# A hybrid decoder layer: hand-overs and last job by token tile, columns by transposes, halved final stores

## What is computed

```python
mod = silu(c) @ w_ada + b_ada          # six groups of D: shift1, scale1, gate1, shift2, scale2, gate2
u = x * (1 + scale1) + shift1
h = u @ w_in                            # inputs of three branches (conv, gated DeltaNet, attention) and their gates
m = sum(sigmoid(g_i) * (y_i @ P_i))     # merge of the three branches
x = LN(alpha * x + gate1 * (m @ w_o))   # first norm, then
u = x * (1 + scale2) + shift2           # (ln1's gain and bias and scale2, shift2 are folded into one multiply and add)
h = relu(u @ w_ff1) ** 2                # D_FF = 8192
x = LN(alpha * x + gate2 * (h @ w_ff2)) # the output
```

## Time and profile before

| what | us |
|---|---|
| median of 3 runs (2622.71, 2624.74, 2627.75) | 2624.74 |
| the profiled execution, its own time | 2627.94 |
| its span (first to last event in the trace) | 2626.2 |
| PE busy / DVE busy / ACT busy / POOL busy | 2554.2 / 1721.4 / 1172.5 / 84.4 |
| mean granted clock of PE | 0.983 |
| HBM traffic | 534.68 MB read, 205 GB/s over the span |

### The profile page before, as it was taken

One profiled execution on the slowest core, in us unless ns is written; L12 is line 12 of the kernel. 1 busy time (PEld: TensorE's weight loads), 2 busy tenths in 40 slices (PEclk: granted clock), 3 DMA queues, 4 the chain that ended last, 5 costly groups with the idle time before them and its releaser, 6 DMA issues.

```text
span 2626.2 us, 33584 instructions
## 1 busy us (share of the span) xinstructions
PE 2554.2 (97%) x12200; PEld 2086.3 (79%) x12200; DVE 1721.4 (66%) x2318; ACT 1172.5 (45%) x1453; POOL 84.4 (3%) x89
## 2 busy tenths in 40 slices
PE   7888999999999999999999999999999999999997
PEld 3567888788878887888788888878788888888886
DVE  4677766786678757776667667766665645546556
ACT  2146354635463545535444434434454354453442
POOL 0001010101001100110000000000000000000000
PEclk8799999999999999999999999999999999999999
DMA  9865657656666567556787877877565665666654
GB/s 311 308 202 161 179 170 223 184 175 181 199 208 176 161 190 237 168 148 181 235 263 239 268 255 238 265 234 254 155 183 190 226 184 191 191 186 194 186 190 137
DMA packets 300174, 540.05 MB, mean 206 GB/s; under 512 B 39152, under 2 KB 44784, under 8 KB 298736
## 3 DMA queue, kind: packets, MB, share of 16 engines
q1 hardware_dynamic: 270752, 522.29, 63.7%
q10 hardware_dynamic: 29264, 15.68, 2.0%
HBM read 534.68 MB, written 3.21 MB: 205 GB/s over the span
## 4 chain that ended last, share of the span: by engine, by line
PE 50%; DVE 1%; ACT 0%; DMA 0%; issue 0%; DVEq 0%; ACTq 0%
PE acc L1725 49%; PE bank L1728 1%; PE bank L1725 0%; DVE z_lo L1095 0%; DVE w_lo L1110 0%; DMA raw<-in_w_in 0%; DVE xr L1101 0%; DVE x L1101 0%; DVE macc L1101 0%; ACT w_hi L647 0%; DVE stats L1594 0%; DVE xr L1095 0%; DVE ff_part L1095 0%; DVE gated L1557 0%; DVE merged L1559 0%
## 5 line engine op out<-in xcount | busy, mean ns | idle before, releaser
L1110 DVE TENSOR_TENSOR w_lo<-raw,w_hi 128x1024 fp32r<-128x1024 f32 x800 | 982.3, 1228 | 686.6 <-ACT w_hi L647 642.4
L647 ACT ACTIVATE w_hi<-raw 128x1024 fp32r<-128x1024 f32 x792 | 835.7, 1060 | 1134.8 <-PE acc L1725 823.1
L1725 PE MATMUL acc<-w_hi,u_hi 128*128 128x512 f32 x2304 | 921.7, 400 | 21.9 <-DVE w_lo L1110 18.7
L1725 PE MATMUL acc<-w_hi,u_lo 128*128 128x512 f32 x2304 | 903.0, 392 | 0.0
L1725 PE MATMUL acc<-w_lo,u_hi 128*128 128x512 f32 x2304 | 902.1, 392 | 0.0
L1725 PEld LDWEIGHTS acc<-w_hi,u_hi 128*128 128x128 f32 x2304 | 435.6, 189 | 120.5 <-DVE w_lo L1110 22.9
L1725 PEld LDWEIGHTS acc<-w_hi,u_lo 128*128 128x128 f32 x2304 | 435.3, 189 | 93.0
L1725 PEld LDWEIGHTS acc<-w_lo,u_hi 128*128 128x128 f32 x2304 | 436.2, 189 | 86.2 <-issue 1.0
L1725 PE MATMUL acc<-w_hi,z_hi 128*128 128x512 f32 x896 | 350.9, 392 | 3.7 <-DVE mod L1095 3.7
L1725 PE MATMUL acc<-w_hi,z_lo 128*128 128x512 f32 x896 | 349.4, 390 | 0.0
L1725 PE MATMUL acc<-w_lo,z_hi 128*128 128x512 f32 x896 | 349.3, 390 | 0.0
(11 more groups left out here) (247 smaller groups left out, 1470.1 us busy)
## 6 DMA issues: line engine op xcount, KB each, us to landing
raw<-in_w_in SPq DMA_DIRECT2D x416, 512.0 KB, 4.5
raw<-in_w_ff SPq DMA_DIRECT2D x256, 512.0 KB, 4.3
raw<-in_w_ada SPq DMA_DIRECT2D x192, 512.0 KB, 4.7
raw<-in_w_branch_a SPq DMA_DIRECT2D x32, 512.0 KB, 4.8
raw<-in_w_branch_b SPq DMA_DIRECT2D x32, 512.0 KB, 4.9
raw<-in_w_branch_c SPq DMA_DIRECT2D x32, 512.0 KB, 4.8
raw<-in_w_o SPq DMA_DIRECT2D x32, 512.0 KB, 4.7
IT<-decay_d ACTq DMA_DIRECT2D x8, 512.0 KB, 6.5
```

The costliest lines, as they stand in the source:

```text
L647: a.activation(w_hi[:, u % PARTS, :, :], raw[:, rl % RAWS, :, :], ACT.Copy).then_inc(hi_ready.sem, 1)
L1110: v.tensor_tensor(w_lo[:, u % PARTS, :, :], raw[:, rl % RAWS, :, :] if src is None else src, w_hi[:, u % PARTS, :, :], ALU.subtract).then_ ...
L1725: return t_.matmul(dst, lhsT, rhs, start=start, stop=stop)
```

## The change

- `mod` groups, 8 in the passes and 8 in the merge: PE transposes the four 128 x 128 blocks of `macc` (four `turn`), and DVE sums 128 values for each of 4 columns (`sum_turned`, a `tensor_reduce` into the new tile `mcol`) ahead of the addition. The groups of the first stage (`first_columns`) stay as they are.
- `gate_rows` uses `turn` too. The second `gate_rows` moves from after the last W_o job to slot 24 of the stage (AT_GATE2).
- Merge: the wait for `mod_set` moves behind the next slots.
- First pass: `load_decay` moves ahead of the exponential of the heads; AT_DECAY is 48 instead of 50.
- `by_tile` replaces `last_units`: all 8 units of the job first for token tile 0, then for tile 1. It is used for the last W_o job, the first FF1 job and the last FF2 job. Its units find their halves by `weights(n)`: for two jobs from the last W_o job on, the first 4 units of each lie in `zw_hi`, `zw_lo` (over z_hi, z_lo, unused then); in the last FF2 job in `uw_hi`, `uw_lo` (over u_hi, u_lo). `slot_free(n)` lets these units be converted 4 units earlier.
- The hand-over goes by token tile: `turn_xhat(m, n)` transposes 4 k tiles of one token tile into a bank (tile 0 during the second half of the last W_o job, tile 1 during the first half of the first FF1 job), `make_u2` on ACT makes all of u2 (4 activations of 128 x 128 per group), `make_lo` on DVE its lower half.
- Tail: the last two passes over the columns and the stores are done in two halves of 1024 columns.

```diff
+N_OUT = (J_OUT + NCH - 1) * UPJ
+N_LAST = (J_FF + FFQ * FF_JOBS - 1) * UPJ
...
-AT_SMALL, AT_SUMS, AT_DECAY = KT + 1, 40, 50
+AT_GATE2 = 24
+AT_SMALL, AT_SUMS, AT_DECAY = KT + 1, 40, 48
...
+        uw_hi = sb("uw_hi", [P, PARTS, UK, NC], F32R, at=u_at)
+        zw_hi = sb("zw_hi", [P, PARTS, UK, NC], F32R, at=tmp_at)
...
+        def weights(n):
+            if N_OUT <= n < N_OUT + 2 * UPJ and n % UPJ < PARTS:
+                return zw_hi[:, n % PARTS, :, :], zw_lo[:, n % PARTS, :, :]
+            if N_LAST <= n < N_LAST + PARTS:
+                return uw_hi[:, n % PARTS, :, :], uw_lo[:, n % PARTS, :, :]
+            return w_hi[:, n % PARTS, :, :], w_lo[:, n % PARTS, :, :]
+
+        def slot_free(n):
+            return n + 1 - (PARTS if N_OUT <= n < N_OUT + 2 * UPJ or n >= N_LAST else 0)
...
                 if i == 0:
+                    act.wait_ge(decay_out.sem, 16)
+                    load_decay()
                     act.wait_ge(N["decay_left"].sem, 1)
                     activate(heads[:, 4, :, :], heads[:, 4, :, :], ACT.Exp, "heads_made", 1)
...
-                if i == 0:
-                    act.wait_ge(decay_out.sem, 16)
-                    load_decay()
...
+            out_to(AT_GATE2 + 1)
+            gate_rows(1, gate2_b, 0)
+            gate_rows(1, gate2_b, 2)
...
+            def make_u2(m, n):
+                g = NCH * m + n
+                act.wait_ge(N["xhat_turned"].sem, g + 1)
+                if m:
+                    act.wait_ge(N["u2_lo"].sem, n + 1)
+                for q in range(BPC):
+                    k = BPC * n + q
+                    activate(u2[n][:, q, :], bank[n][:, q * P:(q + 1) * P], ACT.Identity, *(("u2_made", g + 1) if q == BPC - 1 else ()),
+                             scale=lnc[:, 0, k:k + 1], bias=lnc[:, 1, k:k + 1])
+                o.after()
+                activate(u_hi[:, BPC * n:BPC * (n + 1), m * P:(m + 1) * P], u2[n][:, :, :], ACT.Copy, "u2_hi", g + 1)
+
+            first_ff = NCH * UPJ
+            out_unit(first_ff)
             root(0, 0)
+            out_unit(first_ff + 1)
+            out_unit(first_ff + 2)
+            make_u2(0, 0)
+            out_unit(first_ff + 3)
+            make_u2(0, 1)
+            out_unit(first_ff + 4)
+            make_u2(0, 2)
             root(0, 1)
+            out_unit(first_ff + 5)
+            make_u2(0, 3)
+            out_unit(first_ff + 6)
+            out_unit(first_ff + 7)
+            for n in range(NCH):
+                make_u2(1, n)
...
+            def sum_turned(n, b):
+                o.do(v.tensor_reduce(mcol[:, n % 2, :], b[:, :].rearrange("p (b c) -> p b c", c=P), mybir.AxisListType.X, ALU.add))
+                o.after()
+                return mcol[:, n % 2, :]
...
+            residual(0)
+            inverse_root(0, 0)
+            for n in range(NCH):
+                xhat(0, n)
+            for n in range(3):
+                out_unit(first_ff + n)
+            make_lo(0, 0)
+            out_unit(first_ff + 3)
+            make_lo(0, 1)
+            residual(1)
+            out_unit(first_ff + 4)
+            make_lo(0, 2)
+            inverse_root(0, 1)
+            xhat(1, 0)
+            xhat(1, 1)
+            out_unit(first_ff + 5)
+            make_lo(0, 3)
+            out_unit(first_ff + 6)
+            xhat(1, 2)
+            xhat(1, 3)
+            out_unit(first_ff + 7)
+            make_lo(1, 0)
...
+                for h in range(2):
+                    cs = slice(h * D // 2, (h + 1) * D // 2)
+                    stt(xr[:, m, cs], xr[:, m, cs], aggr[:, m, 0:1], ln_g[:, cs], ALU.subtract, ALU.mult)
+                    o.after()
+                    stt(x1[:, m, cs], xr[:, m, cs], rstd[:, m:m + 1], ln_b[:, cs], ALU.mult, ALU.add, "out_made", 2 * m + h + 1)
...
-            def last_units(n, dst, left):
+            def by_tile(n, dst, j, left, side):
                 hi, lo = left
                 for m in range(MT):
                     ms = slice(m * P, (m + 1) * P)
-                    for v in range(PARTS):
+                    for v in range(UPJ):
                         if m == 0:
                             pe.wait_ge(lo_ready.sem, n + v + 1)
+                        if n == J_FF * UPJ and v % 2 == 0:
+                            pe.wait_ge(N["u2_lo"].sem, NCH * m + v // 2 + 1)
...
+                        side(m, v)
...
-                        last = mm(bank[MOD_BANK[n]][:, b:b + 1], macc[:, n % 2, b * P:(b + 1) * P], ones[:, 0:1])
+                        last = turn(bank[MOD_BANK[n]][:, b * P:(b + 1) * P], macc[:, n % 2, b * P:(b + 1) * P])
...
                 if n == MMODS - 1:
-                    pe.wait_ge(N["mod_set"].sem, FIRST_GROUPS + n)
                     for t in range(6):
                         next_slot((MERGES - 1) * 4 * UPJ + KT + 2 * t + 2 - count[0])
+                        if t == 0:
+                            pe.wait_ge(N["mod_set"].sem, FIRST_GROUPS + n)
                         turn_merged(t)
...
-                        last = mm(bank[n][:, b * P:(b + 1) * P], mod[:, k:k + 1].broadcast_to([P, P]), ident[:, :])
+                        last = turn(bank[n][:, b * P:(b + 1) * P], mod[:, k:k + 1].broadcast_to([P, P]))
...
+            def out_side(m, v):
+                if (m, v) == (1, 3):
+                    pe.wait_ge(N["gate_made"].sem, 2 * NCH)
+                if m and 3 <= v < 3 + NCH:
+                    turn_xhat(0, v - 3)
+
+            by_tile(N_OUT, 1, (J_OUT + NCH - 1) // 2 + 1, (u_hi, u_lo), out_side)
+
+            def ff_side(m, v):
+                if m == 0 and v in (5, 7):
+                    turn_xhat(1, v - 5)
+                    turn_xhat(1, v - 4)
+
+            by_tile(J_FF * UPJ, 0, J_FF // 2 + 1, (u_hi, u_lo), ff_side)
...
+                        by_tile(N_LAST, 1, (J_FF + FFQ * FF_JOBS - 1) // 2 + 1, (z_hi, z_lo), lambda m, v: None)
```

More of the change, by code:

```diff
@@ L253, in layer_program @@
         w_lo = sb("w_lo", [P, PARTS, UK, NC], F32R)
+        u_at = top[0]
         u_hi = sb("u_hi", [P, KT, S], F32R)
@@ L1044, in _ @@
                     o.begin(i, 60)
-                count = [0]
+                count = [0 if i else UK * (UPJ - LEAD)]
                 next_slot = slots(i, FF_JOBS * UPJ, J_FF * UPJ, FF_JOBS * UPJ, R_FF, plain_place, count)
                 if i == 0:
[L1048 to L1062, removed]
                     o.begin(0, 60)
@@ L1079, in _ @@
                                  *(("h_hi", j + 1) if h else ()))
-                while count[0] < FF_JOBS * KT - (2 * LEAD if i == FFQ - 1 else 0):
+                while count[0] < (FF_JOBS - (2 if i == FFQ - 1 else 0)) * KT:
                     next_slot()
+                if i == FFQ - 1:
+                    for u in range((FF_JOBS - 2) * UPJ + LEAD, FF_JOBS * UPJ):
+                        r = i * FF_JOBS * UPJ + u
+                        hi_unit(J_FF * UPJ + r, u, 16 * ((R_FF + r) // RAWS + 1), u)
                 o.end(FFQ if i == FFQ - 1 else 0)
@@ L1590, in _, with variance @@
             o.begin(0, 200)
-            def normalise(which, m, cols):
+            def variance(m, which=0):
                 o.do(v.bn_stats(stats[:, m, NCH - 1, :], xr[:, m, cols]))
@@ L1617, in _, with residual @@
                 o.after()
-            out_to(AT_HALF + 2)
+            out_unit(first_ff - 1)
             cols = slice((NCH - 1) * NC, NCH * NC)
-            for m in range(MT):
+            def residual(m):
                 if m:
@@ L1683, in _ @@
                         break
-                    while count[0] < (j + 1) * KT:
-                        next_slot()
+                    if i < FFQ - 1 or j < FF_JOBS - 2:
+                        while count[0] < (j + 1) * KT:
+                            next_slot()
+                    else:
+                        for u in range(j * UPJ + LEAD, FF_JOBS * UPJ - 1):
+                            lo_unit((i * FF_JOBS + J_FF) * UPJ + u, u, u)
                     job_wait(dve, i * FF_JOBS + (J_FF + j))
@@ L1697, in _ @@
                 if i == FFQ - 1:
-                    while count[0] < FF_JOBS * KT - 2 * LEAD:
-                        next_slot()
+                    u = FF_JOBS * UPJ - 1
+                    lo_unit((i * FF_JOBS + J_FF) * UPJ + u, u, u)
                 o.end(FFQ if i == FFQ - 1 else 0)
@@ L2130, in _ @@
                 for b in range(BPC):
-                    last = mm(bank[n % 4][:, b:b + 1], macc[:, n % 2, b * P:(b + 1) * P], ones[:, 0:1])
+                    last = turn(bank[n % 4][:, b * P:(b + 1) * P], macc[:, n % 2, b * P:(b + 1) * P])
                 last.then_inc(N["mcol_summed"].sem, 1)
@@ L2159, in _, with turn_xhat @@
             gate_rows(0, 2 * KT)
[L2160 to L2161 removed]
+            next_slot(AT_GATE2 - count[0])
             gate_rows(1, 5 * KT)
[L2163 to L2174 removed]
+            next_slot((NCH - 1) * KT - count[0])
+            def turn_xhat(m, n):
+                pe.wait_ge(N["xhat_made"].sem, NCH * m + n + 1)
+                if m:
```

(8 more changed lines are left out.)

139 lines of the change are left out of this document (56 added, 83 removed).

## The result

| what | before | after |
|---|---|---|
| median of 4 runs, us | 2623.72 (2621.99 to 2627.75) | 2600.82 (2600.38 to 2601.19) |
| profiled execution, its own time | 2627.94 | 2600.64 |
| its span | 2626.2 | 2598.9 |
| mean granted clock of PE | 0.983 | 0.986 |

The ratio is 0.9909, 95% interval 0.9893 to 0.9924: faster by 22.9 us. The forecast was 2598.5, in a range of 2590.5 to 2608.

The account below looks back on a forecast made before the run. PE, busy 97% of 2626.2 us, was taken to bound the kernel, almost all of it matmul issue. The terms summed to -26.3 us: 2601.6 for a profiled execution, 2598.5 for a median, range 2590.5 to 2608.

Parts of the forecast that it names:

- C: Mod columns by transposes in passes and merge: 0.46 us less PE per group against 0.7 more DVE, sum -3.4 us.
- A: First pass, earlier decay load: normalised KC ready about 3.9 us sooner, PE's hole cut to 2 us, worth -5.5 us.
- D: Gate rows by transposes instead of fp32 products: first gate 3.49 to 1.75 us on PE, worth -1.75 us.
- E: Hand-over, last W_o job and first FF1 job by token tile: job start to first ReLU shortened, worth -7.3 us.
- I take no fall: First pass: PE's clock would not drop behind the remaining 2 us hole before KC.
- B: Merge, wait for DVE's mod columns moved: removes PE's 3.68 us wait and 1.6 of slow clock, -5.3 us.
- Rival 1: Passes: DVE takes over, reductions delay late weight units; total gain only -19.5, so 2605.2 us; chance 0.12.
- Rival 2: Mod columns, gate rows, hand-over: transposes save nothing on PE; total gain only -15.9, so 2608.8 us; chance 0.07.
- Rival 3: Rows of transposes count as idling, three clock falls of 1.6 us; total -21.5, so 2603.2 us; chance 0.05.
- Rival 4: Hand-over becomes a ping-pong of PE and ACT waits, +22 us there; total -4, so 2620.5 us; chance 0.03.
- Rival 5: By-tile jobs: weight supply starves first tiles, units 6.6 us in series; slower, about 2661 us; chance 0.03.
- F: Tail, last job by token tile with half passes and half stores: tile 1 starts sooner, last store shorter, -3.1 us.

Follow-up runs that it names:

- the repair: The changed kernel with all DVE subtractions of the decays in the first pass done before the next two weight units; 2598.61 us.

## Why the prediction was right, and where it was not

**The total.** The terms summed to -26.3; the profiled pair moved by 27.3, of which 1.9 belongs to no edit, so the change itself gave 25.4. The median came 2.3 us above the forecast: I carried the profiled execution's excess of 3.2 us over to the new kernel as a constant, while the new kernel's profile lay at its median. That the sum came so close is in part luck: C gave 1.0 more than forecast, while A fell 1.3 short, D and E 0.7 and the last job 0.5.

**A, 1.3 too high.** The failed step is "I take no fall". The hole was 2 us as forecast, and the clock fell to half for some 3 us. The ground for that step was one execution, and a row that shows too little: the 2.48 us idle in 170 to 175 are the part inside the window of a single wait of 2.94 us, behind which the clock falls in most runs (last section). The run with the same hole and no fall prices it: between KC and the macc group PE is there 1.5 us sooner, of which 0.8 is given back at the next tight unit (it waits 1.32 instead of 0.73), so 0.7 net. The other 0.6 is DVE: I had w_lo ready at 257.3, its subtraction only started at 257.29, and it was ready at 258.5. Expecting DVE to be 6 us earlier behind KC was too much (its last work ahead of the reduction began 4.9 earlier, 254.30 for 259.22); the bound (-3.3 to -8.9) held.

**B** gave 5.42 for 5.3. The undoing showed 6.9, for a reason outside the sum: C lengthens the wait that B removes.

**C.** The late groups gave 0.47 each. The reduction from PSUM took 0.69 us on average over 16, as the one from SBUF that I took for it (0.68), so neither bound was needed. Of the first groups, two cost +0.8 as forecast (+0.7), while the one in pass 4 gained 0.46: two waits there, 0.24 and 0.59, became one of 1.15. The reading behind the term was loose too: PE waits 0.62 us at 540.96 and 0.59 at 1096.39, but at 818.58 only 0.20. Rival 1 (2605.2) is out for C, since the second groups cost nothing on DVE and the first ones 1.2 us where the forecast itself had 2.1; only A moved towards its 3.3.

**D and E, 0.7 too high together.** Gate rows: 1.66 us for 16 transposes, for 1.75 forecast, so -1.83 on the row; a factor of 2.1 in place of the four that the Trainium skill's "TensorE: Matmul & The Clock Gate" (Terms) gives for FP32. By that factor D would have been -2.6, and undoing both gates +5.2; the trace shows 2.9. From job start to ReLU I forecast 48.6 and got 49.1; the two waits read 0.34 us each for 0.6 and 0.8 forecast, but each costs 0.62 by the starts of the matmuls around it, 1.2 in all for 1.4, and one fell in the W_o job itself. In the W_o stage PE needed another 0.45 beside the gate rows, which was not followed. The order by token tile at the hand-over, the largest term, was never undone as a whole; its share is read from one pair of traces.

**F** gave 3.2 for 3.1, and its parts were tried apart: order of units 2.7 (forecast 2.25), halves and stores 0.9 (0.8). They don't add, since where tile 1 waits for DVE the halves also lengthen tile 0's chain. What I had left out is the supply of the last job, +0.5: one wait, recorded at 0.20 us (2575.17), which costs 0.48 between the starts of two matmuls.

**Rivals.** Rival 2 is out: every copied, summed and spread column costs half. Rival 3 is out: the clock was 1.00 over 1785 to 1800 and 1812 to 1825 us, around the runs of 16 transposes, and over all of the hand-over. So the rule of the Trainium skill ("TensorE: Matmul & The Clock Gate", "PE-mode transpose") does not show here, where the runs last under 2 us and matmuls surround them. Rival 4: no chain of single waits arose. Rival 5 was not near: even without the head start PE waits only 2.4 to 2.6 us, once in a job, where the rival had 5.2 for each of four units.

**Open.** 1.9 us of the passes belong to no edit. Single waits for w_lo (0.59 at 456.84 and 0.70 at 734.96 before) are missing after, and return in other runs whose stream there is the same. They vary by run; why was not tried. The run with the columns by products with ones has the second of them at 1.36 us.

## What to carry to other kernels

Look at the instruction next in line, not only at the data: an operand that comes earlier gains little while its user stands behind a unit of another engine, and two slots in the order turned 1.7 us of gain into 4.8. Price a saving on PE twice where its cost goes to the engine that feeds PE: the same edit gave 0.47 us where DVE idled and cost 0.8 where DVE was late, and moving the sums 8 slots later turned that round. A hole of 2 us or more on PE mostly costs more than itself: where the clock fell behind a hole of 2.0 to 4.8 us, 1.3 to 2.2 us came on top. Holes of 0.78 to 1.51 us in the kernel after left the clock at 1.00, so a hole that a change can't close may be worth narrowing further (not tried here: the repair closed it). And don't take the clock of one execution for the kernel's.

## What was not expected of the hardware

The clock is not settled by the length of the hole before it. Eight runs (after and seven experiments) have a hole of 2.01 or 2.02 us for KC behind the same work: in seven the granted clock fell behind it (mean 0.88 over 218 to 232 us), in one it stayed at 1.00. What tips it there stays open.

A longer hole does not settle it either. All 13 traces have a wait of 2.93 to 2.97 us for w_lo near 170 us, behind work that no edit touches. Over the 6 us behind it the mean clock was 0.72 in nine of them and 1.00 in four (before, decay load as before, AT_DECAY 50, last job's first units for both tiles). Before and after, with the columns of the earlier trace rows:

```profile
172.48 0.50 PE L1725 MATMUL acc<-w_hi,u_hi 128*128 128x512 f32 x1 [2.94 <-DVE w_lo L1110]
...
171.53 0.50 PE L1798 MATMUL acc<-w_hi,u_hi 128*128 128x512 f32 x1 [2.95 <-DVE w_lo L1148]
```

```profile
172.48:178.48 6.00, 5.80 (x25) 4.45 (x25) 5.20 (x12) 1.21 (x2) 0.00 (x0) 1.00 0.59 175
171.53:177.53 6.00, 6.00 (x19) 4.79 (x20) 5.19 (x12) 1.06 (x1) 0.00 (x0) 0.72 0.60 174
```

What PE did 6 us earlier differs: a shorter wait for w_lo stands there, of 0.34 to 0.43 us in the four and of 0.56 to 1.35 us in the nine. That it decides is not shown. The fall costs some 1.3 us, by which the kernel before gains on the kernel after in this place, outside every term. Behind the other holes of 2.42 to 6.14 us that were read, all from 220 us on, the clock fell each time.
